# Cross attention's value products as three products of rounded halves, with the memory's low parts made on GpSimd in four pieces

## The chip, the cores and the metric

The kernel runs on one core of a Trainium2 chip. The metric is the device time of one execution in microseconds; the time of a kernel is the median of its runs. The engines named below are TensorE (PE, with its weight loads PEld), VectorE (DVE), ScalarE (ACT), GpSimd (POOL) and SyncE (SP), which issues the DMAs.

## What is computed

Two transformer blocks over 512 tokens of width 1024. The change sits in the first block, in attention over a memory of 256 rows with 4 heads of 256 columns, and beside the output projection of the mixing layer that runs just ahead of it:

```python
h = h + jnp.concatenate([ret, fox], axis=-1) @ w_out[l]
h = h + memory_cross_attention(rmsnorm(h, g_xattn[l]), mem, ...)

def memory_cross_attention(hn, mem, w_xq, w_xkv, g_mem, g_xq, g_xk, w_xo):
    q = rmsnorm((hn @ w_xq).reshape(B, T, 4, 256), g_xq)
    k, v = jnp.split(rmsnorm(mem, g_mem) @ w_xkv, 2, axis=-1)
    k = rmsnorm(k.reshape(B, M, 4, 256), g_xk)
    logits = jnp.einsum('bthd,bmhd->bhtm', q, k) * 256 ** -0.5
    p = jax.nn.softmax(logits, axis=-1)
    o = jnp.einsum('bhtm,bmhd->bthd', p, v).reshape(B, T, D_MODEL)
    return o @ w_xo
```

Everything is float32. The last einsum, probabilities by values, is what the change rewrites.

## The kernel before

Activations stand with features on the partitions: a chunk is 128 features by 512 tokens, eight chunks make a 1024-wide activation. Weights come as **units**, 128x1024 floats, one unit for each output chunk: SP loads unit u into one of four slots of `raw`, ACT rounds it into `whi` (`high_part`, L674), POOL subtracts to get `wlo` (`low_part`, L555), and PE multiplies. A float32 product is written as three products of rounded (fp32r) halves: `whi` by the activation's high part, `whi` by its low part, `wlo` by its high part (`high_passes` and `low_pass`, L2261, L2262, L2267, 24 matmuls for a unit). `whi` and `wlo` have two slots each. Units are numbered through the whole program: the layer `out` has units 45 to 52, `xq` (queries) 53 to 60, `xo` 61 to 68.

The order on every engine is the order of the text, and semaphores tie the engines together.

**The layer `out`, units 45 to 52.** For each unit c of the layer PE writes bank c % 4. DVE then adds the bank to the residual `h` (L1464), adds the square of the chunk before to `ssum` (L1362) and makes the low part `yl` of the chunk before (L1369). ACT squares the new chunk (L729), makes its high part `yh` (L731), and rounds the next unit (L674). POOL makes each unit's low part after ACT's rounding. Between these, DVE normalises the memory's keys (`memory_key_norm`): a reciprocal (L1977) behind `h` of chunks 2 and 4, and four products `kmem` of 128x256 (L1982) behind chunks 3 and 5. The first unit of `xq`, unit 53, is different from the others: its products come tile by tile (`two_units`, L2235 to L2237), and its first matmul already waits for unit 53's low part on POOL (`lo_ready`).

**The memory's values** `vmem` are 128x2048: two blocks of 128 memory rows, 1024 columns each, copied out of PSUM by ACT at L1190 before `out` begins.

**Cross attention.** Scores of a head go to banks 0 and 1 or 2 and 5. DVE takes the row maxima (L2021), ACT the exponentials (L1236), DVE divides by the sums (L2035), PE transposes the probabilities into banks 3 and 4 (`memory_transposes`, L2884), and ACT copies bank 3 (L1245) and DVE bank 4 (L2042) to `pt_x`. `memory_values` (L2897) multiplies `vmem` by `pt_x` as plain float32, four matmuls for a head, into banks 6 and 7; ACT makes the high part of the result (`memory_out_high`, L1251) and DVE the low part (`memory_out_low`, L2049), which the layer `xo` reads. PE's order is: values of head 0, transposes of 1, scores of 3, values of 1, transposes of 2, four tiles of `xo` (12 matmuls), values of 2, transposes of 3, four tiles of `xo`, values of 3, the rest of the first two units of `xo`.

Of the kernel before, what the change touches and what calls it, by code (L numbers as in the profile page):

```python
# [134 lines left out]
def two_block_kernel(nc, x_t, mem_t, units, ada_rows, c_rows, vectors, tables, decays, out_t):  # L135
# [4 lines left out]
    with ExitStack() as ctx:  # L140
# [3 lines left out]
        def sem(name):  # L144
            return ctx.enter_context(nc.semaphore(name))
# [44 lines left out]
        def at(name, kb, cols, dt=f32, base=arena_at):  # L190
            return nc.alloc_sbuf_tensor_at(name, [P, cols], dt, offset=base + int(kb * 1024))
# [16 lines left out]
        p_x, pt_x = (at("p_x0", 48, 1024), at("p_x1", 56, 1024)), at("pt_x", 52, 1024)  # L208
# [78 lines left out]
        vmem_copied, gate_silu = (sem(n) for n in ("vmem_copied", "gate_silu_product_scaled"))  # L287
        kmem_sq, kmem_sum, kmem_root, kmem_rstd, kmem_done = (
# [263 lines left out]
        def _(pool):  # L552
# [7 lines left out]
            def low_parts(u, end):  # L560

                a, b = -(-u // 4), end // 4
                for v in range(u, 4 * a):
                    low_part(v, v % 4)
                with pool.Fori(a, b) as i:
                    for j in range(4):
                        low_part(4 * i + j, j)
                for v in range(4 * b, end):
                    low_part(v, v % 4)
# [61 lines left out]
            low_parts(2, xo0 + 3)  # L631
# [27 lines left out]
        def _(act):  # L659
# [104 lines left out]
            def residual_layer(name, norm, dst=None, gain=None):  # L764

                def epilogue(g, j):
                    act.wait_ge(resid, RESID[name] + g + 1)
                    norm_chunk(norm, g, j, dst=dst, gain=gain)
                    if norm in SHIFTED:
                        raw_high(norm, (g,))  # L770
                run_layer(name, epilogue, second_ahead=True)
# [433 lines left out]
            residual_layer("out", "xattn", yh, "g_xattn")  # L1205
# [34 lines left out]
            def memory_probabilities_copy(hd):  # L1240

                act.wait_ge(xat.s_tr, hd + 1)
                if hd >= 1:
                    act.wait_ge(xat.s_pv, hd)
                act.activation(xat.pt[:, 0:T], banks[3][:, :], ACT.Copy).then_inc(xat.s_pt_act, 1)  # L1245
# [105 lines left out]
        def _(dve):  # L1351
# [685 lines left out]
            def memory_probabilities_copy(hd):  # L2037

                dve.wait_ge(xat.s_tr, hd + 1)
                if hd >= 1:  # L2040
                    dve.wait_ge(xat.s_pv, hd)
                dve.tensor_copy(xat.pt[:, T:2 * T], banks[4][:, :]).then_inc(xat.s_pt_dve, 1)  # L2042
# [21 lines left out]
            memory_probabilities_copy(0)  # L2064
# [5 lines left out]
            memory_probabilities_copy(1)  # L2070
            memory_out_low(0)
            memory_maxima(3)
            memory_out_low(1)
            memory_probabilities_copy(2)
            memory_normalise(3)
            memory_probabilities_copy(3)
            memory_out_low(2)
            memory_out_low(3)
# [143 lines left out]
        def _(pe):  # L2222
# [654 lines left out]
            def memory_transposes(hd):  # L2877
# [9 lines left out]
                bank_free[3], bank_free[4] = [(xat.s_pt_act, hd + 1)], [(xat.s_pt_dve, hd + 1)]  # L2887

            def memory_values(hd):

                pe.wait_ge(xat.s_pt_act, hd + 1)
                pe.wait_ge(xat.s_pt_dve, hd + 1)
                for d in range(2):
                    take(6 + d)
                    o = (2 * hd + d) * P
                    for kb in range(2):
                        last = mm(banks[6 + d][:, :], vmem[:, kb * D + o:kb * D + o + P], xat.pt[:, kb * T:(kb + 1) * T],  # L2897
                                  start=kb == 0, stop=kb == 1)
                last.then_inc(xat.s_pv, 1)
                bank_free[6] = bank_free[7] = [(xat.s_lo, 2 * hd + 2)]  # L2900
# [339 lines left out]
```

## Time and profile before

| what | value |
|---|---|
| median of 3 runs | 1987.74 us (1986.55 to 1988.45) |
| the profiled execution | 1986.42 us |
| its span in the trace | 1984.6 us |
| PE busy | 1962.6 us, 99% |
| DVE busy | 1242.0 us, 63% |
| POOL busy | 906.5 us, 46% |
| ACT busy | 895.5 us, 45% |
| chain that ended last | 95% on PE |

Times in the rows count from the start of the span. A row of the timeline gives the start, the duration, the engine, the line, what is written and read, how many instructions are merged into it, and in brackets the idle time ahead of it and what ended it. A merged row lasts from the start of its first to the end of its last. Matmuls overlap: the distance between two starts is what one costs PE, and it is shorter than the duration of one.

### The profile page before, as it was taken

The numbers are of one execution on the slowest core, as the hardware profiler recorded it, in microseconds if no ns is written. First come the engines' busy times: TensorE is split into PE (matmuls) and PEld (weight loads), VectorE is DVE, ScalarE is ACT, GpSimd is POOL, SyncE is SP. The second block draws the span as 40 slices with busy tenths as digits, with TensorE's granted clock in tenths as the row PEclk, the third lists the DMA queues.
The fourth block names the chain that finished last, engine by engine and source line by source line (L and its number), as shares of the span: only waits on it lengthen the run. The fifth ranks groups of instructions, "written<-read, shape, count | busy, mean of one in ns | idle before, by whom it ended". The sixth has DMA issues, their size and how long they took to land.

```text
span 1984.6 us, 32388 instructions
## 1 busy us (share of the span) xinstructions
PE 1962.6 (99%) x11598; PEld 1699.2 (86%) x11598; DVE 1242.0 (63%) x1933; ACT 895.5 (45%) x1603; POOL 906.5 (46%) x458
## 2 busy tenths in 40 slices
PE   9999999999999999999999999999999999999998
PEld 7788788878999988899998888887777888999887
DVE  4586875346888787887768773463552347877111
ACT  5234444344566522556652252225663246666322
POOL 3344323326577754544445434443224445444443
PEclk9999999999999999999999999999999999999999
DMA  6253222212333387233339635422222232333331
GB/s 211 82 155 107 84 74 83 77 43 87 105 106 106 116 310 254 94 107 106 106 114 330 246 105 144 115 96 84 67 70 87 85 96 93 109 106 106 103 99 64
DMA packets 67246, 234.71 MB, mean 118 GB/s; under 512 B 7632, under 2 KB 9040, under 8 KB 66640
## 3 DMA queue, kind: packets, MB, share of 16 engines
q1 hardware_dynamic: 66432, 232.29, 35.7%
q8 instruction: 61, 1.00, 0.2%
q10 hardware_dynamic: 720, 1.15, 0.2%
q14 instruction: 33, 0.27, 0.0%
HBM read 225.54 MB, written 2.10 MB: 115 GB/s over the span
## 4 chain that ended last, share of the span: by engine, by line
PE 95%; DVE 3%; ACT 1%; issue 1%; POOL 0%; POOLq 0%; DVEq 0%; ACTq 0%
PE bank L2261 12%; PE bank L2262 12%; PE bank L2267 12%; PE bank L2428 9%; PE bank L2429 9%; PE bank L2432 9%; PE bank L2373 5%; PE bank L2374 5%; PE bank L2379 5%; PE bank L2235 1%; PE bank L2237 1%; PE bank L2236 1%; PE bank L2547 1%; PE bank L2548 1%; PE bank L2555 1%; PE bank L2871 1%
## 5 line engine op out<-in xcount | busy, mean ns | idle before, releaser
L555 POOL TENSOR_TENSOR wlo<-raw,whi 128x1024 fp32r<-128x1024 f32 x233 | 580.6, 2493 | 800.1 <-ACT whi L674 799.8
L674 ACT ACTIVATE whi<-raw 128x1024 fp32r<-128x1024 f32 x233 | 245.9, 1057 | 472.9 <-PE bank L2379 217.3
L2261 PE MATMUL bank<-xh,whi 128*128 128x512 f32 x764 | 302.2, 396 | 0.3 <-DVE proj L1422 0.3
L2262 PE MATMUL bank<-xl,whi 128*128 128x512 f32 x764 | 297.7, 390 | 0.0
L2373 PE MATMUL bank<-hh,whi 128*128 (+1 forms) x480 | 186.9, 389 | 0.7 <-ACT whi L674 0.7
L2374 PE MATMUL bank<-hl,whi 128*128 (+1 forms) x480 | 186.8, 389 | 0.0
L2267 PE MATMUL bank<-xh,wlo 128*128 128x512 f32 x736 | 181.7, 389 | 0.0
L2261 PEld LDWEIGHTS bank<-xh,whi 128*128 128x128 f32 x764 | 143.5, 188 | 34.0 <-issue 3.6
L2262 PEld LDWEIGHTS bank<-xl,whi 128*128 128x128 f32 x764 | 143.5, 188 | 29.6 <-issue 0.7
L2267 PEld LDWEIGHTS bank<-xh,wlo 128*128 128x128 f32 x736 | 138.1, 188 | 28.9
L1745 DVE CUSTOM_DVE_ANT_0 xn<-ada_w,csilu 128x1024 f32<-128x1024 f32 x72 | 134.7, 1870 | 21.2 <-ACT csilu L787 12.6
L586 POOL TENSOR_TENSOR gate_lo<-raw,gate_hi 128x512 fp32r<-128x512 f32 x54 | 87.9, 1628 | 111.3 <-ACT gate_hi L870 111.3
L598 POOL TENSOR_TENSOR up_lo<-raw,up_hi 128x512 fp32r<-128x512 f32 x54 | 92.9, 1720 | 84.0 <-ACT up_hi L878 84.0
L2379 PE MATMUL bank<-hh,wlo 128*128 (+1 forms) x480 | 118.7, 389 | 0.0
L2428 PE MATMUL bank<-s,w_t 128*128 128x256 f32 x432 | 106.5, 281 | 1.6 <-DVE tmp L1637 1.6
L2373 PEld LDWEIGHTS bank<-hh,whi 128*128 128x128 f32 x480 | 90.1, 188 | 19.8 <-ACT whi L674 1.2
L2379 PEld LDWEIGHTS bank<-hh,wlo 128*128 128x128 f32 x480 | 90.0, 188 | 18.9 <-POOL wlo L555 0.3
L2429 PE MATMUL bank<-s,w_t 128*128 128x256 f32 x432 | 106.1, 279 | 0.0
L2429 PE MATMUL bank<-xl,gate_hi 128*128 128x256 f32 x432 | 106.1, 279 | 0.0
L2374 PEld LDWEIGHTS bank<-hl,whi 128*128 128x128 f32 x480 | 90.1, 188 | 18.6
L2428 PE MATMUL bank<-xh,gate_hi 128*128 128x256 f32 x432 | 106.0, 279 | 0.0
L1626 DVE TENSOR_TENSOR w_t<-bank,w_t 128x512 fp32r<-128x512 f32 x108 | 73.8, 686 | 35.1 <-ACT w_t L861 35.1
(404 smaller groups left out, 4662.4 us busy)
## 6 DMA issues: line engine op xcount, KB each, us to landing
raw<-units SPq DMA_DIRECT2D x341, 512.0 KB, 3.5
ada_w<-ada_rows SPq DMA_DIRECT2D x72, 512.0 KB, 5.3
h<-x_t SPq DMA_DIRECT2D x8, 256.0 KB, 5.6
out_t<-h SPq DMA_DIRECT2D x8, 256.0 KB, 2.3
raw<-units SPq DMA_DIRECT2D x4, 256.0 KB, 4.9
mem_in<-mem_t SPq DMA_DIRECT2D x1, 1024.0 KB, 11.2
turned_q<-proj SPq DMA_DIRECT2D x4, 256.0 KB, 5.9
dec<-decays SPq DMA_DIRECT2D x4, 256.0 KB, 4.7
```

The costliest lines, as they stand in the source:

```text
L555: pool.tensor_tensor(wlo[:, j % 2 * UNIT:(j % 2 + 1) * UNIT], raw[:, j * UNIT:(j + 1) * UNIT], whi[:, j % 2 * UNIT:(j % 2 + 1) * UNIT].bit ...
L674: act.activation(whi[:, v % 2 * UNIT:(v % 2 + 1) * UNIT], raw[:, slot * UNIT:(slot + 1) * UNIT], ACT.Copy).then_inc(hi_ready, 1)
L1745: dve.tensor_tensor_reduce(product[:, :], ada_w[:, j * D:(j + 1) * D], csilu[:, :], 1.0, 0.0, ALU.mult, ALU.add, dots[:, j:j + 1]).then_in ...
L2261: mm(bank[:, 0:n], wh, chunk(rhs[0], t, n), start=t == 0, stop=False)
L2262: mm(bank[:, 0:n], wh, chunk(rhs[1], t, n), start=False, stop=False)
L2267: last = mm(bank[:, 0:n], wlo[:, slot * UNIT + t * P:slot * UNIT + (t + 1) * P], chunk(rhs[0], t, n), start=False, stop=t == 7)
L2373: mm(bank[:, :], whi[:, w0:w0 + P], chunk(hh, k0 + kk), start=first and kk == 0, stop=False)
L2374: mm(bank[:, :], whi[:, w0:w0 + P], chunk(hl, k0 + kk), start=False, stop=False)
L2379: done = mm(bank[:, :], wlo[:, w0:w0 + P], chunk(hh, k0 + kk), start=False, stop=False)
L2428: mm(out, w, x[0][t], start=start and t == 0, stop=False, skip_group_check=True)
L2429: mm(out, w, x[1][t], start=False, stop=False, skip_group_check=True)
L2432: last = mm(out, w_lo[:, t * P:(t + 1) * P], x[0][t], start=False, stop=t == 3, skip_group_check=True)
```

## The change

- `vmem` gets rounded halves. ACT makes `vmem_hi` in two copies of 128x1024, behind its work on chunks 1 and 2 of `out`. POOL makes `vmem_lo` (written over `vmem`) in four subtractions of 128x512, one ahead of each of the low parts of units 50 to 53.
- `pt_x` becomes `pt_x_hi` and `pt_x_lo`. ACT copies both banks of the transposes (it copied one), and DVE subtracts twice for each head (it copied once), each time after ACT's copy. Banks 3 and 4 are free again only after DVE's subtraction.
- `memory_values` becomes 12 fp32r matmuls for a head in place of 4 float32 ones: eight with `pt_x_hi`, then four with `pt_x_lo`.
- On DVE the outputs' low parts of heads 0 and 2 now go ahead of the low parts of the probabilities of heads 1 and 3, and the division of head 3 goes ahead of the low parts of head 2.
- `low_parts` handles short ranges without a loop, since the single loop over units 4 to 63 is cut.

```diff
@@ -205,7 +205,8 @@
         qroot, qrec, qvar, row_eps, g_xqk = (es[:, a:b] for a, b in ((0, 16), (16, 32), (32, 48), (48, 52), (52, 54)))
-        p_x, pt_x = (at("p_x0", 48, 1024), at("p_x1", 56, 1024)), at("pt_x", 52, 1024)
+        p_x, pt_x = (at("p_x0", 48, 1024), at("p_x1", 56, 1024)), (at("pt_x_hi", 52, 1024, f32r), at("pt_x_lo", 60, 1024, f32r))
+        vmem_hi, vmem_lo = at("vmem_hi", 64, C * M, f32r), at("vmem_lo", 80, C * M, f32r)
@@ -285,6 +286,7 @@
         vmem_copied, gate_silu = (sem(n) for n in ("vmem_copied", "gate_silu_product_scaled"))
+        vmem_split = sem("vmem_split")
         kmem_sq, kmem_sum, kmem_root, kmem_rstd, kmem_done = (
@@ -560,6 +562,10 @@
                 a, b = -(-u // 4), end // 4
+                if a >= b:
+                    for v in range(u, end):
+                        low_part(v, v % 4)
+                    return
                 for v in range(u, 4 * a):
@@ -628,7 +634,17 @@
             xo0, u0 = L["xo"].u0, L["gu"].u0
-            low_parts(2, xo0 + 3)
+            def memory_value_lows(part):
+
+                pool.wait_ge(vmem_copied, C + part // 2 + 1)
+                cols = slice(part * T, (part + 1) * T)
+                pool.tensor_tensor(vmem_lo[:, cols], vmem[:, cols], vmem_hi[:, cols].bitcast(f32), ALU.subtract).then_inc(vmem_split, 1)
+            ahead = L["out"].u0 + 5
+            low_parts(2, ahead)
+            for part in range(4):
+                memory_value_lows(part)
+                low_parts(ahead + part, ahead + part + 1)
+            low_parts(ahead + 4, xo0 + 3)
             for c in range(7):
@@ -761,13 +777,15 @@
-            def residual_layer(name, norm, dst=None, gain=None):
+            def residual_layer(name, norm, dst=None, gain=None, after=None):
...
                         raw_high(norm, (g,))
+                    if after:
+                        after(g)
                 run_layer(name, epilogue, second_ahead=True)
@@ -1202,7 +1220,11 @@
                 act.activation(banks[4 + n][:, :], banks[4 + n][:, :], ACT.Sqrt, bias=col("eps")).then_inc(kmem_root, 1)
-            residual_layer("out", "xattn", yh, "g_xattn")
+            def memory_value_highs(g):
+                if g in (1, 2):
+                    cols = slice((g - 1) * D, g * D)
+                    act.activation(vmem_hi[:, cols], vmem[:, cols], ACT.Copy).then_inc(vmem_copied, 1)
+            residual_layer("out", "xattn", yh, "g_xattn", memory_value_highs)
@@ -1242,7 +1264,8 @@
                     act.wait_ge(xat.s_pv, hd)
-                act.activation(xat.pt[:, 0:T], banks[3][:, :], ACT.Copy).then_inc(xat.s_pt_act, 1)
+                for kb in range(2):
+                    act.activation(xat.pt[0][:, kb * T:(kb + 1) * T], banks[3 + kb][:, :], ACT.Copy).then_inc(xat.s_pt_act, 1)
@@ -2034,12 +2057,12 @@
-            def memory_probabilities_copy(hd):
-
-                dve.wait_ge(xat.s_tr, hd + 1)
-                if hd >= 1:
-                    dve.wait_ge(xat.s_pv, hd)
-                dve.tensor_copy(xat.pt[:, T:2 * T], banks[4][:, :]).then_inc(xat.s_pt_dve, 1)
+            def memory_probabilities_low(hd):
+
+                for kb in range(2):
+                    dve.wait_ge(xat.s_pt_act, 2 * hd + kb + 1)
+                    cols = slice(kb * T, (kb + 1) * T)
+                    tt(xat.pt[1][:, cols], banks[3 + kb][:, :], xat.pt[0][:, cols].bitcast(f32), ALU.subtract).then_inc(xat.s_pt_dve, 1)
@@ -2061,20 +2084,20 @@
             memory_maxima(1)
-            memory_probabilities_copy(0)
+            memory_probabilities_low(0)
             query_variances(1)
...
             memory_normalise(2)
-            memory_probabilities_copy(1)
             memory_out_low(0)
+            memory_probabilities_low(1)
             memory_maxima(3)
             memory_out_low(1)
-            memory_probabilities_copy(2)
             memory_normalise(3)
-            memory_probabilities_copy(3)
+            memory_probabilities_low(2)
             memory_out_low(2)
+            memory_probabilities_low(3)
             memory_out_low(3)
@@ -2884,18 +2907,26 @@
                 last.then_inc(xat.s_tr, 1)
-                bank_free[3], bank_free[4] = [(xat.s_pt_act, hd + 1)], [(xat.s_pt_dve, hd + 1)]
+                bank_free[3], bank_free[4] = [(xat.s_pt_dve, 2 * hd + 1)], [(xat.s_pt_dve, 2 * hd + 2)]
...
-                pe.wait_ge(xat.s_pt_act, hd + 1)
-                pe.wait_ge(xat.s_pt_dve, hd + 1)
-                for d in range(2):
-                    take(6 + d)
-                    o = (2 * hd + d) * P
-                    for kb in range(2):
-                        last = mm(banks[6 + d][:, :], vmem[:, kb * D + o:kb * D + o + P], xat.pt[:, kb * T:(kb + 1) * T],
-                                  start=kb == 0, stop=kb == 1)
+                if hd == 0:
+                    pe.wait_ge(vmem_split, 4)
+                for kb in range(2):
+                    pe.wait_ge(xat.s_pt_act, 2 * hd + kb + 1)
+                    for d in range(2):
+                        if kb == 0:
+                            take(6 + d)
+                        w0 = kb * D + (2 * hd + d) * P
+                        mm(banks[6 + d][:, :], vmem_hi[:, w0:w0 + P], xat.pt[0][:, kb * T:(kb + 1) * T], start=kb == 0, stop=False)
+                        mm(banks[6 + d][:, :], vmem_lo[:, w0:w0 + P], xat.pt[0][:, kb * T:(kb + 1) * T], start=False, stop=False)
+                for kb in range(2):
+                    pe.wait_ge(xat.s_pt_dve, 2 * hd + kb + 1)
+                    for d in range(2):
+                        w0 = kb * D + (2 * hd + d) * P
+                        last = mm(banks[6 + d][:, :], vmem_hi[:, w0:w0 + P], xat.pt[1][:, kb * T:(kb + 1) * T],
+                                  start=False, stop=kb == 1)
                 last.then_inc(xat.s_pv, 1)
```

POOL, from the end of its loop of low parts on, before. `wlo` is a unit's low part, the loop covers units 4 to 63, and `x_89` belongs to the layer behind `xo`:

```order
L555 TENSOR_TENSOR wlo<-raw,whi 128x1024 [waits hi_ready]
L565 REGISTER_ALU
L565 COMPARE_AND_BRANCH
L555 TENSOR_TENSOR wlo<-raw,whi 128x1024 [waits hi_ready]
L576 TENSOR_TENSOR x_89<-xh,xl 128x512 [waits norm_lo]
```

And now, where the first two low parts are those of units 48 and 49:

```order
L557 TENSOR_TENSOR wlo<-raw,whi 128x1024 [waits hi_ready] x2
L641 TENSOR_TENSOR vmem_lo<-vmem,vmem_hi 128x512 [waits vmem_copied]
L557 TENSOR_TENSOR wlo<-raw,whi 128x1024 [waits hi_ready]
L641 TENSOR_TENSOR vmem_lo<-vmem,vmem_hi 128x512 [waits vmem_copied]
L557 TENSOR_TENSOR wlo<-raw,whi 128x1024 [waits hi_ready]
L641 TENSOR_TENSOR vmem_lo<-vmem,vmem_hi 128x512 [waits vmem_copied]
L557 TENSOR_TENSOR wlo<-raw,whi 128x1024 [waits hi_ready]
L641 TENSOR_TENSOR vmem_lo<-vmem,vmem_hi 128x512 [waits vmem_copied]
L557 TENSOR_TENSOR wlo<-raw,whi 128x1024 [waits hi_ready] x3
```

Four subtractions stand between low parts where none stood.

PE in cross attention, from the values of head 0 to the transposes of head 1, before. Each float32 matmul is one row here and two records in the trace:

```order
L2897 MATMUL bank<-pt_x,vmem 128x512 [waits qn_var,xat_pt_dve,xat_pt_act]
L2897 MATMUL bank<-pt_x,vmem 128x512
L2897 MATMUL bank<-pt_x,vmem 128x512 [waits qn_var]
L2897 MATMUL bank<-pt_x,vmem 128x512
L2884 MATMUL bank<-tab,p_x_63 128x128 [waits xat_pt_dve,xat_pt_act,xat_pn]
```

And now, with the rows that only repeat left out in one place:

```order
L2922 MATMUL bank<-pt_x_hi,vmem_hi 128x512 [waits qn_var,xat_pt_act,vmem_split]
L2923 MATMUL bank<-pt_x_hi,vmem_lo 128x512
...
L2922 MATMUL bank<-pt_x_hi,vmem_hi 128x512 [waits xat_pt_act]
...
L2928 MATMUL bank<-pt_x_lo,vmem_hi 128x512 [waits xat_pt_dve]
L2928 MATMUL bank<-pt_x_lo,vmem_hi 128x512
L2928 MATMUL bank<-pt_x_lo,vmem_hi 128x512 [waits xat_pt_dve]
L2928 MATMUL bank<-pt_x_lo,vmem_hi 128x512
L2907 MATMUL bank<-tab,p_x_63 128x128 [waits xat_pt_dve,xat_pn]
```

The wait for DVE has moved from ahead of the first matmul to ahead of the ninth.

DVE between the maxima of head 3 and the residuals of `xo`, before (`rs` and `p_x_63` are the division of head 3, `yl` the outputs' low parts):

```order
L2049 TENSOR_TENSOR yl<-bank,yh 128x512 [waits xat_hi] x2
L2042 COPY pt_x<-bank 128x512 [waits xat_pv,xat_tr]
L2031 RECIPROCAL rs<-sm 128x4 [waits xat_exp]
L2035 TENSOR_SCALAR p_x_63<-p_x_63,rs 128x256 [waits xat_recip]
L2035 TENSOR_SCALAR p_x_63<-p_x_63,rs 128x256 x3
L2042 COPY pt_x<-bank 128x512 [waits xat_pv,xat_tr]
L2049 TENSOR_TENSOR yl<-bank,yh 128x512 [waits xat_hi] x4
```

And now:

```order
L2072 TENSOR_TENSOR yl<-bank,yh 128x512 [waits xat_hi] x2
L2054 RECIPROCAL rs<-sm 128x4 [waits xat_exp]
L2058 TENSOR_SCALAR p_x_63<-p_x_63,rs 128x256 [waits xat_recip]
L2058 TENSOR_SCALAR p_x_63<-p_x_63,rs 128x256 x3
L2065 TENSOR_TENSOR pt_x_lo<-bank,pt_x_hi 128x512 [waits xat_pt_act] x2
L2072 TENSOR_TENSOR yl<-bank,yh 128x512 [waits xat_hi] x2
L2065 TENSOR_TENSOR pt_x_lo<-bank,pt_x_hi 128x512 [waits xat_pt_act] x2
L2072 TENSOR_TENSOR yl<-bank,yh 128x512 [waits xat_hi] x2
```

The low parts of head 2's probabilities now stand behind the division of head 3.

## Rows read from the trace of the kernel before

**Rows 1.** The page: the span, and PE's busy time and instructions.
```profile
span 1984.6 us, 32388 instructions
PE 1962.6 (99%) x11598; PEld 1699.2 (86%) x11598; DVE 1242.0 (63%) x1933; ACT 895.5 (45%) x1603; POOL 906.5 (46%) x458
```
**Rows 2.** The tile `vmem`: its matmul records, durations in ns, least, median and most.
```profile
L2897 PE MATMUL bank<-pt_x,vmem x32: 590/592/592, 400.8 to 425.7; 128*128 128x512 f32 x32
```
**Rows 3.** Timeline of PE: a low pass, then values and tiles in cross attention.
```profile
339.19 1.98 PE L2267 MATMUL bank<-xh,wlo 128*128 128x512 f32 x8
...
400.82 3.60 PE L2897 MATMUL bank<-pt_x,vmem 128*128 128x512 f32 x8
404.25 1.04 PE L2884 MATMUL bank<-tab,p_x 128*128 128x128 f32 x8
...
415.65 3.59 PE L2897 MATMUL bank<-pt_x,vmem 128*128 128x512 f32 x8
...
422.72 3.59 PE L2897 MATMUL bank<-pt_x,vmem 128*128 128x512 f32 x8
```
**Rows 4.** Timeline of ACT, then of DVE, around the values of head 2.
```profile
412.62 1.09 ACT L1251 ACTIVATE yh<-bank 128x512 fp32r<-128x512 f32 x2
413.25 1.29 DVE L2049 TENSOR_TENSOR yl<-bank,yh 128x512 fp32r<-128x512 f32 x2 [2.85 <-ACT yh L1251]
```
**Rows 5.** Timeline of POOL in the layer `out`: low parts of units 49, 50, 53.
```profile
317.06 2.40 POOL L555 TENSOR_TENSOR wlo<-raw,whi 128x1024 fp32r<-128x1024 f32 x1 [6.76 <-ACT whi L674]
322.50 2.73 POOL L555 TENSOR_TENSOR wlo<-raw,whi 128x1024 fp32r<-128x1024 f32 x1 [3.04 <-ACT whi L674]
...
338.81 2.38 POOL L555 TENSOR_TENSOR wlo<-raw,whi 128x1024 fp32r<-128x1024 f32 x1 [2.70 <-ACT whi L674]
```
**Rows 6.** Timeline of DVE in the layer `out`.
```profile
320.05 0.68 DVE L1362 TENSOR_TENSOR ssum<-ssum,tmp 128x512 f32<-128x512 f32 x1
...
321.31 1.67 DVE L1982 SCALAR_TENSOR_TENSOR kmem<-kmem,es,xn 128x256 f32<-128x256 f32 x4
324.88 0.69 DVE L1464 TENSOR_TENSOR h<-bank,h 128x512 f32<-128x512 f32 x1 [1.90 <-PE bank L2267]
...
326.75 3.35 DVE L1977 RECIPROCAL xn<-bank 128x512 f32<-128x512 f32 x1
...
335.76 0.69 DVE L1464 TENSOR_TENSOR h<-bank,h 128x512 f32<-128x512 f32 x1 [1.90 <-PE bank L2267]
```
**Rows 7.** Timeline of ACT in `out`: the roundings of units 51 and 53.
```profile
326.81 1.04 ACT L674 ACTIVATE whi<-raw 128x1024 fp32r<-128x1024 f32 x1
...
337.69 1.04 ACT L674 ACTIVATE whi<-raw 128x1024 fp32r<-128x1024 f32 x1
```
**Rows 8.** Timeline of PE: the start of unit 51, and of unit 53.
```profile
330.12 0.39 PE L2261 MATMUL bank<-xh,whi 128*128 128x512 f32 x1
...
341.29 0.47 PE L2235 MATMUL bank<-yh,whi 128*128 128x512 f32 x1
```
**Rows 9.** Timeline of DVE and POOL in the layer `gu`; then one of POOL alone.
```profile
561.92 0.70 DVE L1610 TENSOR_TENSOR bank<-raw 128x512 f32<-128x512 f32 x1 [0.26 <-DMA raw<-units]
561.93 1.84 POOL L586 TENSOR_TENSOR gate_lo<-raw,gate_hi 128x512 fp32r<-128x512 f32 x1
...
562.53 1.80 DVE L1611 TENSOR_TENSOR bank<-raw 128x512 f32<-128x512 f32 x1
...
437.05 1.29 POOL L576 TENSOR_TENSOR x<-xh,xl 128x512 f32<-128x512 f32 x1 [0.63 <-DVE xl L1369]
```
**Rows 10.** PE: its first matmuls and its last; then stretches with busy time and granted clock.
```profile
1.32 6.02 PE L2606 MATMUL bank<-idle_rows 128*128 128x512 bf16 x14 [1.32 <-POOL idle_rows L558]
...
1975.41 2.05 PE L2521 MATMUL bank<-tab,rcol 128*128 128x128 f32 x16
...
1978.00:1980.00 2.00, 0.00 (x0) 0.00 (x0) 2.00 (x5) 0.09 (x1) 1.77 (x2) 1.00 0.90 336
1980.00:1982.00 2.00, 0.00 (x0) 0.00 (x0) 0.64 (x1) 0.00 (x0) 0.73 (x1) 0.50 1.04 385
```

## The prediction

> **What bounds the kernel now.** I read the page first. PE is busy 1962.6 of 1984.6 us, 99% [rows 1], and the chain that ended last lies 95% on PE. So a change counts by what it takes from PE's own work and by the waits that it puts into PE's stream; the other engines matter only where PE waits for them. Then I read two stretches of the timeline: cross attention (386 to 431 us), where matmuls are replaced, and the layer `out` (about 308 to 341 us), where the new preparation on ACT and POOL is put. In cross attention PE has no gap: values, transposes and tiles follow one another [rows 3]. In `out` PE has none either, but one handover at its end is tight: POOL's low part of unit 53 runs from 338.81 to 341.19 [rows 5], and the first tile of unit 53 starts at 341.29 [rows 8]. Whatever delays that low part delays PE one for one.
>
> **The products.** Sixteen float32 matmuls show as 32 records [rows 2]. The eight of head 0 start at 400.82 and the transposes behind them at 404.25 [rows 3]: 3.43 us for a head. An fp32r matmul of the same size costs what those of a unit cost: eight in 1.98 us with the last one 0.39 long, so (1.98 - 0.39) / 7 = 0.227 us each [rows 3]. Twelve of them are 2.72 us. The gain is 3.43 - 2.72 = 0.71 us for a head and 2.8 us for four, if PE waits for nothing new.
>
> **Its waits.** ACT copies two banks where it copied one, and DVE subtracts from each. Heads 0, 1 and 3 have room: DVE's subtractions end while PE still runs the first eight matmuls (1.8 us), or during the scores and tiles ahead. Head 2 has not. Two gains of 0.71 bring PE to its values at 415.65 - 1.42 = 414.23 [rows 3], but they write the banks that DVE's `yl` of head 1 reads, and that ends at 413.25 + 1.29 = 414.54 [rows 4]. It does not come earlier with PE, because it follows ACT's `yh`, which follows the exponentials of head 3, which follow DVE's maxima; I worked these through with the extra 0.6 us on DVE, and they stay where they are. PE waits 0.3 us. Then the division of head 3 now stands ahead of the low parts of head 2 on DVE. They are ready at about 416.4 and 417.0, and PE, which wants the first at 414.55 + 1.82 = 416.4, waits another 0.25 us for the pair. So cross attention gives 2.84 - 0.55 = 2.3 us. Values of head 3, before at 422.72, start about 1.6 us earlier, and nothing waits for their low parts.
>
> **The preparation in `out`.** ACT's two copies of 128x1024 cost what a rounding of a unit costs, 1.04 us each [rows 7]. The first falls in an idle stretch. The second stands ahead of the rounding of unit 49 and moves POOL's low part of it from 317.06 [rows 5] to 318.10, still ended 2.4 us before PE wants it. By itself nothing of that reaches PE. The four subtractions on POOL are 1.29 us each [rows 9], and POOL sits idle for 3 us between low parts [rows 5], so they look hidden as well.
>
> They are not, because POOL and DVE block each other. In `gu` DVE starts an addition of two SBUF tensors at 561.92 and POOL one at 561.93. POOL's takes 1.84 instead of 1.29 and ends 1.15 us after DVE's. DVE's next one, queued right behind, starts at 562.53 and takes 1.80: it ends 0.56 us after POOL's [rows 9]. So while one of them runs the other stands still, and at the handover the one that waits goes ahead of the next instruction of the one that ran. DVE's `ssum`, `yl` and `kmem` read two SBUF tensors each; its `h` and the reciprocal read PSUM and pass freely (3.35 us at 326.75 [rows 6], beside POOL).
>
> Now the queue, by these handovers (0.56 us for a blocked DVE operation of 512 columns, an estimated 0.33 for one of 256, since four take 1.67 [rows 6], 1.15 to 1.25 for a blocked piece, 2.25 for a blocked unit's low part: the one of unit 50 ends 325.23, which is 2.25 after `kmem` ends at 322.98 [rows 5, 6]):
> - The low part of unit 49 now ends at 320.5. `ssum`, due 320.05 [rows 6], ends at 321.05; the first piece then runs to 322.2, `yl` to 322.75, the low part of unit 50 to 325.0, one `kmem` to 325.3, the second piece to 326.5, the other three `kmem` to 327.6.
> - Behind them on DVE stands `h` of unit 49. It starts at 327.6 and not at 324.88 [rows 6]: 2.7 us late. ACT's rounding of unit 51 follows it, ends at 330.5 and not 327.85 [rows 7], and PE wants it at 330.12 [rows 8]: PE loses 0.4 us.
> - The reciprocal puts `h` of unit 50 at 332.7. The third piece (to 334.1), `ssum`, `yl`, two `kmem`, the low part of unit 52 (336.1 to 338.4), one `kmem`, the fourth piece (to 340.0) and the last `kmem` alternate. `h` of unit 51 starts at 340.3 and not at 335.76 [rows 6]: 4.5 us late.
> - ACT's rounding of unit 53 moves from 337.69 [rows 7] to 342.2, POOL's low part of it from 338.81 [rows 5] to 343.3, and its end to 345.7. PE starts unit 53 at about 345.7 instead of 341.29 [rows 8]: **4.4 us lost**, 0.4 of it before unit 51 and 4.0 in one idle stretch.
>
> Handovers decided otherwise, or pieces of 1.29 to 1.8 us instead of 1.2, would make this 3.5 to 6 us. If no handover went against DVE, it would be 0. I take 4.4, since the same steps applied to the kernel before give each start in this stretch within 0.2 us. Behind unit 53 PE's work is unchanged.
>
> **The sum** for the profiled execution: 1986.42 (span 1984.6) - 2.3 + 4.4 = 1988.5 us. The median is 1.3 us above that execution, so the forecast is 1987.74 + 2.1 = **1989.8 us**, 0.1% above.
>
> **The clock.** In this trace the granted clock falls once. PE's last matmul ends at 1975.41 + 2.05 = 1977.46; from 1978 to 1980 the clock is 1.00, from 1980 to 1982 it is 0.50 [rows 10], the lower of the levels 2.4 and 1.2 GHz, some 2.5 us after the work ended. Ahead of that PE had only small products, and ahead of unit 53 it has dense ones, which speaks for a longer life of the clock. But an idle stretch of 4 us is as long as the one that made it fall. What it costs then is seen at the start: 14 matmuls of 512 columns take 6.02 us [rows 10], 0.43 each, against 0.227, so 14 x 0.2 = 2.8 us before PE runs at full pace.
> The Trainium skill, TensorE: Matmul & The Clock Gate, section HAM oscillation, says that long idle gaps of TensorE throttle it again and that the work behind the gap then runs at half rate. That speaks against this change; the trace agrees in kind at its end.
>
> **The rivals.**
> - The pieces are hidden: POOL's idle time of 3 us between low parts takes them and DVE catches up. For it: POOL is 46% busy, the pieces are only 1.29 us, and a run of `kmem` may pass as one, as it did beside the low part of unit 50 [rows 5, 6]. Against it: the handover in rows 9. Time: 1987.74 - 2.3 = 1985.4 us, and 1985 to 1987 if part of the delay is left.
> - The delay is as forecast and the idle 4 us let the clock fall. That is the slower side: 1989.8 + 2.7 = 1992.5 us. [...]
> - The change does not do what it says: fp32r products with the new operands cost more than 0.227 us, or the subtractions on DVE come late for every head. Then cross attention gives 0 to 1 us and the sum is 1991 to 1992 us. Against it: the low pass in rows 3, of the same shape and type.
>
> **How the numbers follow.** Forecast 0.40, hidden pieces 0.22, clock 0.28, the rest 0.10. About 0.2% (4.0 us) is what a measurement of this kernel can tell from no change. The forecast and the hidden pieces lie within it; the clock's case straddles its upper edge (1991.7), and I give it 0.23 beyond and 0.05 within; of the rest 0.02 goes to each outside and 0.06 within. So same 0.73, slower 0.25, faster 0.02. The range holds the hidden case at its lower end and the clock's at its upper: 1985.2 to 1993.0.
>
> **What the profile after would show.** `memory_values` as 48 records of 389 ns, 0.227 apart, 10.9 us in place of 13.7, and a gap of 0.3 us on PE ahead of the values of head 2. In `out`: `ssum`, `yl` and `kmem` stretched to 1.2 to 2.9 us beside POOL, `h` of unit 51 some 4.5 us late against the end of PE's unit, PE waiting about 4 us for `wlo` of unit 53. The granted clock in the stretch behind it tells the last two cases apart. The forecast is wrong if that wait is under 1 us, or if the clock falls, or if PE waits in cross attention for DVE at every head.

## The result, and the profile after

The kernel before ran in 1987.18 us and the changed one in 1991.39 us (medians of 22 runs each). The ratio is 1.0019, with a 95% interval of 1.0013 to 1.0025: slower by 2.6 to 5.0 us. The forecast was 1989.8 us, 2.1 above before.

The page of the changed kernel, which answers to [rows 1]: PE is busy for 99% as before, in a span 5.6 us longer.

```profile
span 1990.2 us, 32420 instructions
PE 1964.2 (99%) x11614; PEld 1705.5 (86%) x11614; DVE 1253.2 (63%) x1937; ACT 899.3 (45%) x1609; POOL 913.7 (46%) x462
```

A busy share tells nothing of where 5.6 us went. What tells it is the **shift** of PE: each matmul's start after, less the start of the same matmul before. The heads of the columns are times in the first profile of before. The table has it at six places, in us: ahead of unit 51, at the start of unit 53, 11 us later, behind cross attention, ahead of the last products, and at the last of them. The first column holds what came before the change has any effect: an offset of up to 0.6 us from the first 10 us of the program, and in e1 and e5 another 0.85 and 0.82 us near 237 us, told below. What a stretch costs is the difference of two columns. The rows for the experiments are explained below.

| kernel | 329 | 341 | 352 | 431 | 1970 | end |
|---|---|---|---|---|---|---|
| changed kernel | -0.02 | 4.43 | 5.87 | 3.53 | 3.28 | 6.2 |
| changed kernel, second profile | -0.26 | 3.99 | 5.38 | 3.05 | 4.09 | 5.5 |
| before, second profile | -0.55 | -0.55 | -0.50 | -0.49 | -0.17 | 1.4 |
| e1, pieces in `xq` | 0.45 | 0.46 | 0.47 | -1.84 | -1.84 | -0.6 |
| e2, values alone | -0.08 | -0.07 | -0.04 | -2.37 | -2.92 | -2.9 |
| e3, preparation alone | -0.28 | 3.98 | 5.33 | 5.33 | 5.43 | 6.9 |
| e4, PE kept busy | 0.50 | 4.78 | 4.72 | 2.41 | 3.97 | 5.5 |
| e5, pieces that only write | 0.73 | 0.74 | 0.76 | -1.57 | -2.18 | -2.2 |
| e6, pieces from unit 51 on | -0.26 | 2.04 | 1.99 | -0.35 | -1.11 | 1.5 |
| e7, pieces from unit 52 on | -0.45 | 1.74 | 1.67 | -0.67 | 0.93 | 2.5 |
| e8, DVE's order of before | -0.52 | -0.53 | -0.50 | -1.14 | -1.22 | 1.6 |
| e9, low parts of head 2 first | -0.35 | -0.35 | -0.34 | -2.76 | -3.48 | -3.5 |

So the changed kernel lost 4.45 us up to unit 53, lost 1.44 more behind it (all of it in the first eight matmuls), and won 2.34 in cross attention: 3.55 us in all.

**The layer `out`.** POOL's timeline, which answers to [rows 5]. L641 are the new pieces:

```profile
320.34 1.75 POOL L641 TENSOR_TENSOR vmem_lo<-vmem,vmem_hi 128x512 fp32r<-128x512 f32 x1
322.48 2.40 POOL L557 TENSOR_TENSOR wlo<-raw,whi 128x1024 fp32r<-128x1024 f32 x1 [0.40 <-ACT whi L690]
324.85 1.48 POOL L641 TENSOR_TENSOR vmem_lo<-vmem,vmem_hi 128x512 fp32r<-128x512 f32 x1
...
332.99 1.29 POOL L641 TENSOR_TENSOR vmem_lo<-vmem,vmem_hi 128x512 fp32r<-128x512 f32 x1
335.43 2.39 POOL L557 TENSOR_TENSOR wlo<-raw,whi 128x1024 fp32r<-128x1024 f32 x1 [1.15 <-ACT whi L690]
337.78 1.47 POOL L641 TENSOR_TENSOR vmem_lo<-vmem,vmem_hi 128x512 fp32r<-128x512 f32 x1
343.27 5.12 POOL L557 TENSOR_TENSOR wlo<-raw,whi 128x1024 fp32r<-128x1024 f32 x2 [4.02 <-ACT whi L690]
```

DVE's timeline beside it, which answers to [rows 6]:

```profile
320.85 1.78 DVE L1392 SCALAR_TENSOR_TENSOR yl<-h,vec,yh 128x512 fp32r<-128x512 f32 x1
322.55 4.85 DVE L2005 SCALAR_TENSOR_TENSOR kmem<-kmem,es,xn 128x256 f32<-128x256 f32 x4
327.32 0.68 DVE L1487 TENSOR_TENSOR h<-bank,h 128x512 f32<-128x512 f32 x1
...
333.00 1.83 DVE L1385 TENSOR_TENSOR ssum<-ssum,tmp 128x512 f32<-128x512 f32 x1
...
335.42 4.91 DVE L2005 SCALAR_TENSOR_TENSOR kmem<-kmem,es,xn 128x256 f32<-128x256 f32 x4
340.25 0.67 DVE L1487 TENSOR_TENSOR h<-bank,h 128x512 f32<-128x512 f32 x1
```

Four `kmem` took 1.67 us before and take 4.85 and 4.91 now, each time with a unit's low part and a piece of POOL between them. `h` of unit 51 follows them on DVE, and so it starts at 340.25 and not at 335.76. Then come ACT's rounding of unit 53 and POOL's low part of it (343.27 above), and PE, at the start of unit 51 and at that of unit 53:

```profile
342.16 1.99 ACT L690 ACTIVATE whi<-raw 128x1024 fp32r<-128x1024 f32 x2
...
330.70 0.47 PE L2284 MATMUL bank<-xh,whi 128*128 128x512 f32 x1 [0.44 <-ACT whi L690]
...
345.72 0.76 PE L2258 MATMUL bank<-yh,whi 128*128 128x512 f32 x1 [3.89 <-issue]
346.29 0.63 PE L2259 MATMUL bank<-yl,whi 128*128 128x512 f32 x1
346.71 0.63 PE L2260 MATMUL bank<-yh,wlo 128*128 128x512 f32 x1
...
349.11 0.40 PE L2260 MATMUL bank<-yh,wlo 128*128 128x512 f32 x1
349.35 0.40 PE L2258 MATMUL bank<-yh,whi 128*128 128x512 f32 x1
```

Two things are to be seen. PE idled for 3.89 us, and behind that the starts of its matmuls are 0.43 us apart (346.29 to 346.71), from 349.11 on 0.23. The windows of this stretch say why. Their columns are the stretch, its length, the busy time of PE, PEld, DVE, ACT and POOL, the granted clock, and DMA:

```profile
342.00:344.00 2.00, 0.00 (x0) 0.00 (x0) 2.00 (x4) 2.00 (x3) 0.73 (x1) 1.00 0.00 0
344.00:346.00 2.00, 0.28 (x1) 0.31 (x2) 2.00 (x1) 1.27 (x3) 2.00 (x2) 0.87 0.00 0
346.00:348.00 2.00, 2.00 (x6) 1.52 (x6) 2.00 (x2) 0.00 (x0) 2.00 (x1) 0.50 0.58 170
348.00:350.00 2.00, 2.00 (x8) 1.63 (x7) 1.61 (x2) 0.00 (x0) 0.40 (x1) 0.77 0.50 135
350.00:352.00 2.00, 2.00 (x10) 1.63 (x9) 0.00 (x0) 0.00 (x0) 0.00 (x0) 1.00 0.58 219
```

The granted clock was 0.50, the level of 1.2 GHz, from about 345.5 to 348.9. The Trainium skill, TensorE: Matmul & The Clock Gate, section HAM oscillation, says that idle gaps of TensorE throttle it and that the matmuls behind them run at half rate. The trace agrees: 0.43 against 0.23 us.

**Cross attention.** PE's timeline, which answers to [rows 3]: the values of head 0, the transposes behind them, and the values of head 2 behind the tiles of `xo`.

```profile
406.50 0.58 PE L2922 MATMUL bank<-pt_x_hi,vmem_hi 128*128 128x512 f32 x1
...
409.46 1.04 PE L2907 MATMUL bank<-tab,p_x 128*128 128x128 f32 x8
...
419.91 0.39 PE L2260 MATMUL bank<-yh,wlo 128*128 128x512 f32 x1
420.42 0.47 PE L2922 MATMUL bank<-pt_x_hi,vmem_hi 128*128 128x512 f32 x1
```

The shift falls by 0.66 us over head 0, 0.70 over head 1, 0.23 over head 2 and 0.74 over head 3. At head 2 PE waits: 420.42 is 0.51 behind the matmul ahead of it, where 0.23 is the rule.

**The end of the program.** PE's last products, which answer to the last matmuls in [rows 10]:

```profile
1976.09 2.68 PE L3158 MATMUL bank<-tab,tmp 128*128 128x1 f32 x16
1978.63 1.63 PE L3164 MATMUL bank<-xh,whi 128*128 128x512 f32 x3
1980.06 3.62 PE L2544 MATMUL bank<-tab,rcol 128*128 128x128 f32 x16
```

The last group took 2.05 us before. Here the granted clock was 0.50 from about 1977 on, among small products and ahead of the end of the work. That is 2.9 us of the 6.2 at the end of the table's first row, and whether the change has a part in it was to be tested.

### The profile page after: what moved, and what is told of

The parts are those of the page before. It is cut to its first block, busy times and chain, and to the rows that moved or that the text cites. A ratio compares the mean times of both kernels' runs of the same rounds, so it can differ in the third digit from the quotient of the medians.

```text
span 1990.2 us, 32420 instructions
## 1 busy us (share of the span) xinstructions
PE 1964.2 (99%) x11614; PEld 1705.5 (86%) x11614; DVE 1253.2 (63%) x1937; ACT 899.3 (45%) x1609; POOL 913.7 (46%) x462
## 4 chain that ended last, share of the span: by engine, by line
PE 93%; DVE 4%; ACT 1%; issue 1%; POOL 0%; DMA 0%; SPq 0%; POOLq 0%; DVEq 0%; ACTq 0%
PE bank L2284 12%; PE bank L2285 12%; PE bank L2290 11%; PE bank L2451 9%; PE bank L2455 9%; PE bank L2452 8%; PE bank L2396 5%; PE bank L2397 5%; PE bank L2402 5%; PE bank L2258 1%; PE bank L2260 1%; PE bank L2259 1%; PE bank L2570 1%; PE bank L2578 1%; PE bank L2571 1%
```

## The experiments

My theory: (1) POOL and DVE block each other when both read SBUF tensors, DVE with two of them; (2) this delays unit 53; (3) PE's idle stretch lets the clock fall; (4) the new products and DVE's new order give 2.3 us and have no part in the loss. Rivals: the loss is POOL's added time as such; it comes from the new products; the fall of the clock is chance.

### One half of the change at a time

e2 has the new values without POOL's pieces, and multiplies by the high halves in place of the low ones. e3 has the preparation, and the values of before.

```diff
e2
-            for part in range(4):
-                memory_value_lows(part)
-                low_parts(ahead + part, ahead + part + 1)
-            low_parts(ahead + 4, xo0 + 3)
+            low_parts(2, xo0 + 3)
...
-                        mm(banks[6 + d][:, :], vmem_lo[:, w0:w0 + P], xat.pt[0][:, kb * T:(kb + 1) * T], start=False, stop=False)
+                        mm(banks[6 + d][:, :], vmem_hi[:, w0:w0 + P], xat.pt[0][:, kb * T:(kb + 1) * T], start=False, stop=False)
e3 (against the changed kernel)
...
-                for kb in range(2):
-                    act.activation(xat.pt[0][:, kb * T:(kb + 1) * T], banks[3 + kb][:, :], ACT.Copy).then_inc(xat.s_pt_act, 1)
+                act.activation(xat.pt[:, 0:T], banks[3][:, :], ACT.Copy).then_inc(xat.s_pt_act, 1)
...
-            def memory_probabilities_low(hd):
+            def memory_probabilities_copy(hd):
...
```

> The changed kernel without the subtractions on POOL: the low halves of the memory's values are left out, and the product that should read them reads the high halves again, so that PE's work keeps its size. It shows what the twelve fp32r matmuls for each head and their waits are worth alone. Blocking theory: ratio 0.9988, 2.4 us under the kernel before, PE starts unit 53 at 341.3 us. If ACT's two copies in the layer out cost something by themselves, unit 53 starts later than that by up to 1 us.

> The kernel before with the preparation alone: ACT's two copies and POOL's four subtractions in the layer out, and the float32 product of before (it reads what the subtractions leave, so the high halves of the values are left out of the result). Blocking theory: PE starts unit 53 at 345.7 us, 4.4 later than before, then runs up to 3.4 us at the lower clock; the median is 5 to 6.5 us above the kernel before, ratio 1.0025 to 1.0033. If the loss of the changed kernel sits in cross attention or behind it, this one is within 1 us of the kernel before.

e2: 1984.19 us, ratio 0.9987 (0.9978 to 0.9996). e3: 1993.43 us, ratio 1.0036 (1.0023 to 1.0050). In the table e2 has nothing at unit 53 and wins 2.33 in cross attention; e3 loses 4.26 and then 1.35, and wins nothing. The halves add up to the whole (-2.33 + 5.61 = 3.28 us against 3.55), so the loss is the preparation's. Since e2 keeps ACT's two copies and is not late at unit 53, it is that of POOL's four pieces.

### The pieces in another place

```diff
e1
-            ahead = L["out"].u0 + 5
+            ahead = L["xq"].u0 + 2
```

> The changed kernel with one number changed: the four subtractions on POOL stand ahead of the low parts of units 55 to 58 and not of 50 to 53, so in the layer xq, where DVE's work is copies out of PSUM. If the loss in the layer out comes from POOL and DVE blocking each other, it goes: PE starts unit 53 at 341.3 us as in the kernel before, no clock falls there, and the gain in cross attention (2.4 us in the trace of the changed kernel) is kept, so the median is 2.4 us under the kernel before, ratio 0.9988. If the loss comes from the work itself, which is still all there (four pieces of 1.3 us on POOL, two copies of 1.05 us on ACT), the loss moves with it and the time stays 1 to 4 us above the kernel before.

1985.45 us, ratio 0.9991 (0.9982 to 1.0000). The same four subtractions, five units later and away from `kmem`, cost nothing: three of them take their 1.29 us and one 1.74 (345.2 to 363.1 us), the shift at 352 is that at 329, and cross attention wins 2.31. POOL's added time as such is no cost in this place. The interval reaches 1.0000, so the median alone doesn't show that e1 is faster than before; its trace does. One thing was not expected. The offset of 0.45 was -0.40 at 230 us: the granted clock fell at about 236.8 us in attention of the mixing layer, which no theory had named:

```profile
236.00:238.00 2.00, 2.00 (x12) 1.28 (x9) 2.00 (x2) 0.00 (x0) 2.00 (x1) 0.69 0.00 0
238.00:240.00 2.00, 2.00 (x10) 1.91 (x10) 2.00 (x6) 0.00 (x0) 0.34 (x1) 0.50 0.22 35
```

### Does POOL's reading do it?

e5 puts a memset of 128x1024 where each subtraction stood, so that POOL writes and doesn't read. Each memset waits for both of ACT's copies. The low halves are left out of the product (high halves stand in).

```diff
e5
...
-                pool.tensor_tensor(vmem_lo[:, cols], vmem[:, cols], vmem_hi[:, cols].bitcast(f32), ALU.subtract).then_inc(vmem_split, 1)
...
+                pool.memset(vmem[:, half], 0.0).then_inc(vmem_split, 1)
...
```

> The changed kernel with each of POOL's four subtractions replaced by a fill of 128x1024 with zeros, at the same places in POOL's order. The fills read nothing from SBUF. The low halves of the memory's values are left out, and their product reads the high halves again. Two readings of the loss are told apart. If it is POOL's time (four more operations between the low parts), the fills delay them as the subtractions do and PE starts unit 53 near 345.7 us. If it is that DVE's operations with two SBUF operands and POOL's operations that read SBUF stand still for each other, DVE is not held up by a fill: ssum and yl beside it keep 0.68 and 0.75 us, kmem is held up at most by the low part of unit 50 itself, and PE starts unit 53 at 341.3 to 342 us, so the median is 1.5 to 2.5 us under the kernel before. The Trainium skill, SBUF — State Buffer, section Who interferes with whom, says that a DVE instruction with two SBUF inputs contends with a GpSimd one that reads SBUF and not with one that only writes it, which would give the second outcome.

1984.29 us, ratio 0.9987 (0.9977 to 0.9996), with 0.01 us lost up to unit 53. The median is 2.7 us under before, a little more than the 1.5 to 2.5 expected. POOL, and DVE beside it:

```profile
323.23 2.56 POOL L557 TENSOR_TENSOR wlo<-raw,whi 128x1024 fp32r<-128x1024 f32 x1 [1.20 <-ACT whi L693]
...
331.64 0.95 POOL L644 MEMSET vmem<- 128x1024 f32 x1
...
322.26 3.80 DVE L2008 SCALAR_TENSOR_TENSOR kmem<-kmem,es,xn 128x256 f32<-128x256 f32 x4
...
331.67 0.68 DVE L1388 TENSOR_TENSOR ssum<-ssum,tmp 128x512 f32<-128x512 f32 x1
332.26 0.74 DVE L1395 SCALAR_TENSOR_TENSOR yl<-h,vec,yh 128x512 fp32r<-128x512 f32 x1
332.93 1.66 DVE L2008 SCALAR_TENSOR_TENSOR kmem<-kmem,es,xn 128x256 f32<-128x256 f32 x4
```

`ssum` and the memset run at the same time, each at its own pace; in the changed kernel the same `ssum`, started 0.01 us behind a subtraction, took 1.83 us. The second four `kmem` are back at 1.66 us. The first four still take 3.80 us, since a unit's low part, which reads SBUF as before, falls between them; that makes `h` of unit 49 0.4 us late and nothing behind it. The pieces are 0.95 us long at the same places of POOL's queue, against 1.29 for an unblocked subtraction. The shorter length alone doesn't explain a loss of nothing, since `ssum` starts 0.03 us behind the memset and isn't held at all. The blocking comes with POOL's reading. The Trainium skill, SBUF — State Buffer, section Who interferes with whom, says that a DVE instruction with two SBUF inputs contends with a GpSimd instruction that reads SBUF and not with one that only writes. The runs agree on both halves.

### Fewer pieces ahead of unit 53

```diff
e6
-            ahead = L["out"].u0 + 5
+            ahead = L["out"].u0 + 6
e7
-            ahead = L["out"].u0 + 5
+            ahead = L["out"].u0 + 7
```

> The changed kernel with the four subtractions one unit later, ahead of the low parts of units 51 to 54. Handover theory, worked through with the steps of the prediction: PE starts unit 53 about 1.1 us later than the kernel before (342.4 us) in place of 4.4, because the low part of unit 50 is ready after the first four products of the keys have passed; no lower clock behind it. A theory by which POOL's or DVE's total work decides gives 4 us or more, as for the changed kernel.

> The changed kernel with the four subtractions two units later, ahead of the low parts of units 52 to 55. Handover theory: the first piece meets ssum, yl and the second run of key products; PE starts unit 53 about 2.3 us later than the kernel before (343.5 us), more than with the pieces from unit 51 on (1.1 us), although more of them now lie behind unit 53. A theory by which the work ahead of unit 53 decides gives less than with unit 51.

One run each: 1987.27 and 1988.26 us. Unit 53 is 2.30 us late in e6 and 2.19 in e7. For e7 that is about the expectation, for e6 it is twice. The order of the two, e7 later than e6, didn't come, so this pair doesn't tell the handovers from a count of pieces by the totals. The rows do: three pieces ahead of unit 53 cost as much as two, because in both the second group of `kmem` decides. In e6:

```profile
333.09 4.84 DVE L2005 SCALAR_TENSOR_TENSOR kmem<-kmem,es,xn 128x256 f32<-128x256 f32 x4
337.85 0.68 DVE L1487 TENSOR_TENSOR h<-bank,h 128x512 f32<-128x512 f32 x1
...
343.33 0.47 PE L2258 MATMUL bank<-yh,whi 128*128 128x512 f32 x1 [2.43 <-issue]
```

In e7 the same four take 4.83 us, from 332.79. Both have the low part of unit 52 and a piece between the `kmem`. My working by handovers missed this one in e6, though in the changed kernel it met all. So such a working can be off by a microsecond, here by half of the loss, where a start near a handover decides which instruction goes first. In both, PE idled for 2.43 and 2.32 us ahead of unit 53 and the clock stayed at 1.00 behind it (windows of 342 to 346).

### The clock behind the idle stretch

e4 adds four float32 matmuls whose result nobody reads ahead of unit 53, and else is the changed kernel.

```diff
e4
+            take(6)
+            for _ in range(4):
+                mm(banks[6][:, :], mean_d, chunk(h, 0), start=True, stop=True)
```

> The changed kernel with four idle float32 matmuls of 512 columns (0.86 us each, 3.4 us together, into a bank that nothing reads) ahead of PE's wait for unit 53. They fit into the idle stretch of 3.9 us. If the lower clock behind unit 53's start comes from that idle stretch, the granted clock stays at 1.00 there and the median is 1.5 us under the changed kernel's, some 2.7 us above the kernel before, ratio 1.0013. If the clock falls for another reason, the time is that of the changed kernel, ratio 1.0019 to 1.0021.

1989.36 us, ratio 1.0008 (0.9999 to 1.0017). Its PE:

```profile
342.18 3.59 PE L2941 MATMUL bank<-h,tab 128*128 128x512 f32 x8
346.07 0.47 PE L2258 MATMUL bank<-yh,whi 128*128 128x512 f32 x1 [0.30 <-issue]
346.85 0.39 PE L2258 MATMUL bank<-yh,whi 128*128 128x512 f32 x1
```

Unit 53 is about as late as in the changed kernel (4.28 us), and nothing is lost behind it (4.78 to 4.72): work that nobody needs kept the clock up here. By the ratios the median is 2.2 us under the changed kernel's, where 1.5 was expected; the two intervals overlap, so it is the trace that shows the effect. The second profile of the changed kernel asked the other question, whether the fall comes in each execution, and the second one of before, what the end of the program does without the change.

> The changed kernel as it is, a second profile. My theory of the loss: unit 53 starts 4.4 us late in every execution, the clock falls behind its idle stretch in every execution (7 matmuls at 0.427 us, 1.4 to 1.5 us), and where the clock falls among the last small products is chance. So between unit 51 and unit 60 this profile agrees with the first one within 0.2 us, and at the end of the program it may differ by up to 3 us. Rival, the fall behind unit 53 is chance as well: then this profile shows none there in about half the cases, and the shift against before stays at 4.4.

> The kernel before as it is, a second profile. No fall of the clock near 341 us under either theory, since PE has no idle stretch there. My theory of the end: the fall among the last small products comes by chance in this kernel too, so the last 16 small products (2.05 us in the first profile) may take up to 3.6 us here. Rival, the changed kernel alone has it ahead of the last products: then they take 2.05 us again.

They are single runs of 1991.26 and 1987.26 us. The changed kernel again, behind an idle stretch of 3.68 us:

```profile
345.28 0.76 PE L2258 MATMUL bank<-yh,whi 128*128 128x512 f32 x1 [3.68 <-issue]
...
1979.50 3.42 PE L2544 MATMUL bank<-tab,rcol 128*128 128x128 f32 x16
```

Its windows behind the idle stretch, with the granted clock as the third number from the end:

```profile
346.00:348.00 2.00, 2.00 (x7) 1.51 (x6) 2.00 (x1) 0.00 (x0) 1.96 (x1) 0.50 0.76 238
```

The last products of PE in the second profile of before, where nothing fell at 341:

```profile
1975.24 3.67 PE L2521 MATMUL bank<-tab,rcol 128*128 128x128 f32 x16
```

All three profiles with the idle stretch (changed kernel twice, e3) have the fall behind unit 53, at 1.44, 1.39 and 1.35 us; none of the other ten has one there. Up to unit 53 the second profile lost 4.25 us, the first 4.45, within the 0.2 expected. The fall at the end is another matter. The kernel before pays 1.6 us for it in this profile and had paid nothing in the first. Of the 13 profiles nine pay 1.2 to 2.9 us there (last two columns of the table), with and without the change. So the first is an effect of the change, and the second comes with and without it; what decides about it in one execution is open.

### DVE's new order in cross attention

Both have the pieces in `xq`, as e1. e8 puts DVE's order of before back; e9 moves one line.

```diff
e8
...
-            memory_out_low(0)
             memory_probabilities_low(1)
+            memory_out_low(0)
...
-            memory_normalise(3)
             memory_probabilities_low(2)
-            memory_out_low(2)
+            memory_normalise(3)
             memory_probabilities_low(3)
+            memory_out_low(2)
e9
-            memory_normalise(3)
             memory_probabilities_low(2)
+            memory_normalise(3)
```

> The kernel of e1 (pieces in the layer xq) with DVE's calls in the order of the kernel before: low parts of the probabilities of heads 1 and 3 ahead of the outputs' low parts of heads 0 and 2, and those of head 2 ahead of the division of head 3. It shows what the reordering is worth. Worked through with the durations of the trace: PE waits 1.2 us ahead of the values of head 1 and 0.6 us ahead of those of head 3, and no longer at head 2's low products; cross attention takes 1.25 us longer than in e1. If the order does not matter, it takes as long.

> The version with the four subtractions in xq, and DVE's order in cross attention changed at one place: the low parts of head 2's probabilities go ahead of the division of head 3. Nothing is left out. My theory: with the subtractions in xq nothing of the preparation reaches PE, so this is cross attention's gain alone. Worked through the handovers between ACT, DVE and PE, the wait ahead of the values of head 2 stays (0.25 to 0.3 us), the transposes of head 3 do not come late, and the whole is 0.24 us shorter than with the division first. Time 1984.5 to 1985.5 us where before is 1987.1, ratio 0.9987 (+-0.0008). Rival, the division's place matters because head 3's transposes are next on PE: then this is 0.3 to 0.6 us longer than with the division first, ratio 0.9993.

e8 (one run, 1987.45 us) wins 0.64 us in cross attention where e1 wins 2.31. It waits at two heads:

```profile
408.59 0.47 PE L2922 MATMUL bank<-pt_x_hi,vmem_hi 128*128 128x512 f32 x1 [1.00 <-DVE yl L2072]
...
422.21 0.47 PE L2922 MATMUL bank<-pt_x_hi,vmem_hi 128*128 128x512 f32 x1 [0.64 <-DVE yl L2072]
```

Both waits are for banks 6 and 7, which DVE's `yl` of the head before still reads. By the shift, head by head, e8 is 1.28 us behind e1 at head 1 and 0.89 at head 3, and 0.50 ahead of it at head 2, where e1 waits and e8 doesn't: 1.67 us in all, where 1.25 was expected. The new order is most of what makes the products pay. e9: 1984.06 us, ratio 0.9985 (0.9976 to 0.9994), and 2.42 us in cross attention: 0.1 more than e1, not the 0.24 that I had worked out, but not less either, as the rival had it. The 1.4 us between the medians of e9 and e1 are more than their traces explain, and the two intervals overlap. e9 is faster than the kernel before by 2.9 us, clear of noise, and by the ratios some 7 us faster than the changed one.

## Where the prediction was right and where it was wrong

- **What bounds the kernel, and the tight handover:** right. PE waited for unit 53's low part, one for one.
- **The products** (2.84 us) and **the waits** (0.55): 2.34 us net, forecast 2.3. The gap ahead of head 2 was there, 0.28 us. The new order's worth, which I had worked in and not priced by itself, is 1.67 us (e8).
- **The queue in `out`:** `h` of unit 49 at 327.32 (327.6 forecast), PE's loss ahead of unit 51 0.60 (0.4), `h` of unit 51 at 340.25 (340.3), ACT's rounding at 342.16 (342.2), the low part at 343.27 (343.3), PE at 345.72 (345.7). The rule read off [rows 9], that the waiting engine goes ahead of the next instruction of the other, carried all six starts within 0.3 us. That doesn't make it sure at each place: the same working gave 1.1 us for e6, where 2.30 was measured. The rival of hidden pieces fell by this, and e5 shows its cause.
- **The clock:** here the forecast failed, and by its own sign: it had named a fall of the clock as what would make it wrong. I gave the fall behind unit 53 less than its absence (0.28 against 0.40), since PE's work ahead of it is dense where it had been thin in [rows 10]. The idle stretch was the better sign: behind 3.68 to 3.89 us of it the clock fell three times in three. The rival's size was wrong too. I priced 14 matmuls at half rate, from the start of the program, at 2.8 us and put 2.7 into the sum; here seven ran so, and it cost 1.4.
- **The rest:** forecast +2.1, with the clock's 1.4 added +3.5, and the trace has +3.55 without the end of the program. The medians differ by 4.2, and the interval of 2.6 to 5.0 us holds both; the 0.6 left isn't explained. At the end the lower clock took up to 2.9 us in one execution; [rows 10] have it behind the last product, where it costs PE nothing, and I had no term for it falling earlier.

So the time came out slower as forecast, by twice the amount (4.2 against 2.1 us): the forecast's mechanism as worked out, and on top of it a rival's, of which only half of its price came. That the time stayed inside the range doesn't show the forecast's sum right.

## What to carry to other kernels

Work put into idle time of GpSimd was free here where nothing tight depended on a VectorE operation with two SBUF inputs beside it (e1, e9), and cost 4.45 us on TensorE where something did. So look for what stands behind VectorE's operation in its queue, and follow it to TensorE. An idle stretch that a delay opens on TensorE costs its own length, and can cost the clock behind it: 1.4 us more behind 3.68 to 3.89 us of idle time, nothing more behind 2.43 and 2.32 us. With the new operations five units later, and one line moved on VectorE, the same change turns from 0.2% slower to 0.15% faster (e9).

## What the runs showed of the hardware

- VectorE with two SBUF inputs and GpSimd reading SBUF took turns here. Four products of 128x256 on VectorE went from 1.67 to 4.85 us, with two subtractions of GpSimd between them; a memset of GpSimd (0.95 us) beside `ssum` (0.68 us) cost neither anything.
- The granted clock falls without an idle stretch of that size as well: among small products at the end of the program, in nine of 13 profiles, for 1.2 to 2.9 us, and in two (e1, e5) near 237 us, among products of 128 to 384 columns behind an idle time of 1.55 us, for 0.85 and 0.82 us. The other eleven passed the same work at 1.00. Falls of this size can make up much of the spread between the runs of one kernel (4.3 us over the 22 of before); the profiles are too few to show that they do.
- They are not all of it. Between 431 and 1970 us the shift moves by -0.8 to +1.6 us with the granted clock at 1.00 all the time. In e4 and in the second profile of the changed kernel 1.56 us of that come between 880 and 1040 us, evenly, as if each product took 1% longer; in e7 1.6 us come so behind 1690 us. The cause is open.
